# Conditioning and projection in one block, a third buffer of query weights, and another split of the 128 expert groups

## What is computed

```python
def reference(...):
    sh1, sc1, g1, sh2, sc2, g2 = split(c @ w_ada + b_ada, 6)
    h = rms(x, norm1_g) * (1 + sc1) + sh1
    q, k, v, logf, u = in_proj(h @ w_in)             # QK norm, log sigmoid, GLU
    a_out = forgetting_attention(q, k, v, cumsum(logf))
    c_out = silu(layernorm(causal_depthwise_conv(u, 31 taps)))
    x1 = x + g1 * (concat(a_out, c_out) @ w_o)
    h2 = rms(x1, norm2_g) * (1 + sc2) + sh2
    q = (h2 @ w_query).reshape(n, 8, 2, 128)          # 8 heads, two halves
    s = einsum(q, sub_keys)                           # 2 x 128 keys a head
    i1, i2 = top16(s[:, :, 0]), top16(s[:, :, 1])
    e = top16 of the 16 x 16 sums                     # 16 of 16384 experts, a head
    act = gelu(einsum(h2, expert_u[e]))
    y = x1 + g2 * einsum(softmax(top) * act, expert_v[e])
```

## Time and profile before

| what | value |
|---|---|
| runs | 3864.44, 3870.56, 3872.29 us (median 3870.56) |
| the profiled execution | 3873.22 us, its span 3871.5 us |
| busy: PE, DVE, ACT, POOL | 3115.4, 2471.7, 1550.2, 1283.3 us |
| mean granted clock of PE | 0.908 of full speed |
| DMA | 1291.75 MB in 299720 packets, mean 334 GB/s |
| gathers (q0) | 1124.27 MB, 72.3% of the 16 engines' span |
| SP's DMAs (q1) | 164.51 MB, 12.9% |
| first product of block 0's scores | 652 us |
| scores of blocks 4, 5, 6 begin at | 1920, 2293, 2660 us |

### The profile page before, as it was taken

How to read it: one execution, slowest core, us unless ns; L and a number is a source line. 1 busy time by engine, 2 the same in 40 slices (tenths; PEclk the granted TensorE clock), 3 DMA queues, 4 the chain that set the end, 5 groups by cost and what they waited for, 6 DMA issues and landing times.

```text
span 3871.5 us, 44083 instructions
## 1 busy us (share of the span) xinstructions
PE 3115.4 (80%) x11624; PEld 1421.8 (37%) x11624; DVE 2471.7 (64%) x6411; ACT 1550.2 (40%) x4275; POOL 1283.3 (33%) x1139
## 2 busy tenths in 40 slices
PE   8699976578887887788688868887887788757877
PEld 2466742333342243224332433343334333411341
DVE  0222323488588677767776777587668766856785
ACT  0234411246425533543355345534552555233423
POOL 0000030034334343444344334443343334344433
PEclk9699987699998998899899989998998899979989
DMA  8211152389999999999999999999999999989998
GB/s 317 86 47 41 41 200 96 132 320 399 367 376 366 414 404 375 371 413 407 371 401 409 408 355 404 408 401 378 400 398 403 341 407 405 380 338 418 417 377 355
DMA packets 299720, 1291.75 MB, mean 334 GB/s; under 512 B 39270, under 2 KB 135414, under 8 KB 163124
## 3 DMA queue, kind: packets, MB, share of 16 engines
q0 software_dynamic: 156672, 1124.27, 72.3%
q1 hardware_dynamic: 142780, 164.51, 12.9%
HBM read 1271.34 MB, written 17.79 MB: 333 GB/s over the span
## 4 chain that ended last, share of the span: by engine, by line
DMA 34%; PE 21%; DVE 14%; issue 7%; ACT 5%; SPq 1%; POOL 1%; DVEq 0%; POOLq 0%; ACTq 0%
DMA ring<-experts_dram,idxc 22%; DMA wq<-w_query_dram 12%; PE YY L1670 12%; DVE ring L1515 5%; PE M L1651 4%; PE TT L1657 3%; DVE yac L1262 2%; SPq L1021 1%; ACT gw L1229 1%; ACT dg L1237 1%; ACT L1227 1%; DVE yac L1436 1%; PE SS L1546 1%; ACT ga L1227 1%; POOL ring L1108 1%
## 5 line engine op out<-in xcount | busy, mean ns | idle before, releaser
L1670 PE MATMUL YY<-ring,dg 128*64 128x512 f32 (+1 forms) x4224 | 1804.1, 655 | 486.0 <-ACT dg L1237 463.3
L1108 POOL DMA_INDIRECT ring<-experts_dram,idxc x1056 | 1233.4, 1168 | 1810.3 <-PE YY L1670 1608.0
L1515 DVE CUSTOM_DVE_ANT_0 ring<-ring,h2c 128x1024 f32<-128x1024 f32 x1056 | 1273.3, 1226 | 551.6 <-DMA ring<-experts_dram,idxc 542.2
L1670 PEld LDWEIGHTS YY<-ring,dg 128*64 128x64 f32 (+1 forms) x4224 | 502.1, 145 | 1576.3 <-ACT dg L1237 831.2
L1227 ACT ACTIVATE ga<-act 128x1 f32<-128x1 f32 x1056 | 210.6, 199 | 911.5 <-DVE act L1515 909.1
L1651 PE MATMUL M<-fT,wq 128*128 128x128 f32 (+1 forms) x2304 | 310.2, 299 | 96.3 <-DMA wq<-w_query_dram 96.3
L1237 ACT ACTIVATE dg<-fold,gw 128x64 f32<-128x64 f32 x1024 | 356.0, 348 | 51.0 <-ACT gw L1229 2.6
L1651 PEld LDWEIGHTS M<-fT,wq 128*128 128x128 f32 x2304 | 297.4, 213 | 155.7 <-DMA wq<-w_query_dram 122.4
L1229 ACT ACTIVATE gw<-ga,gc 128x1 f32<-128x1 f32 x1056 | 311.0, 295 | 35.1 <-ACT ga L1227 1.0
L1262 DVE SCALAR_TENSOR_TENSOR yac<-win,cw,yac 128x128 f32<-128x128 f32 x960 | 262.9, 346 | 2.5 <-issue 2.5
L1188 ACT ACTIVATE qh<-M 128x256 f32<-128x256 f32 x64 | 24.5, 383 | 462.4 <-PE M L1651 462.4
(11 more groups left out here) (305 smaller groups left out, 2385.9 us busy)
## 6 DMA issues: line engine op xcount, KB each, us to landing
wq<-w_query_dram SPq DMA_DIRECT2D x72, 1024.0 KB, 27.0
wa<-w_ada_dram SPq DMA_DIRECT2D x12, 2048.0 KB, 7.9
ring<-experts_dram,idxc POOLq DMA_INDIRECT x1056, 13.7
w_in<-w_in_dram SPq DMA_DIRECT2D x1, 10272.0 KB, 34.1
kh<-kT_scratch SPq DMA_DIRECT2D x16, 264.0 KB
xb<-x_prompt_dram SPq DMA_DIRECT2D x8, 512.0 KB, 5.3
t_xb<-x_prompt_dram SPq DMA_DIRECT2D x8, 512.0 KB, 11.1
w_o<-w_o_dram SPq DMA_DIRECT2D x8, 512.0 KB, 5.5
```

What stands on the lines that cost most here:

```text
L1108: pool.indirect_dma_start(ring[:, k % RING, :], None, I["experts"], bass.IndirectOffsetOnAxis(idxc[:, k:k + 1], 0)).then_inc(g_in[k % RING ...
L1515: v.tensor_tensor_reduce(out=u, in0=u, in1=h2, scale=1.0, scalar=0.0, op0=ALU.mult, op1=ALU.add, accum_out=act8[:, k % RING:k % RING + 1]) ...
L1670: mm = pe.matmul(YY[o, half * 512:(half + 1) * 512], dg[:, k % DG, 0:w], ring[:, k % RING, D + half * 512:D + (half + 1) * 512], start=(k ...
```

## The change

There are three parts.

1. `condition` and `project` become one block, `front`. `condition` now returns pieces which `front` puts into each engine's stream. Its PSUM tiles are those of the projection (A[0] to A[4]), its row buffer is `sqq`, its gate buffers are `qTb` and `kTb`. The loads of `w_in` are cut: 8 parts for q, k, v and forget logits (0.79 MB each) stand between the last 8 chunks of `w_ada`, the part for GLU (4.2 MB) behind them. The norm of the sampled rows stands ahead of the conditioning. The gates are now transposed as 9 rows (16 transposes for the 32 products), the spreading into `gS` is gone, and a DMA repeats a gate's one row to 128 rows (from one SBUF partition) or a sample's row to 4. PE waits, ahead of the first q product, until DVE has copied the gates out of PSUM; ACT waits, ahead of its first write to `qTb`, until they are stored.
2. A third buffer for `wq`. It shares its memory (`shared`) with the two `kh` buffers. A load now waits for the product three heads before; that of head 2 waits for the block's last scores, and the next block's prefetch of keys for the product of head 5.
3. `PLAN`: 36 groups stand beside attention (were 50), 29 beside the middle (as before), 63 beside routing (were 49). Behind `write_indices` stand 4 + 3 + 2 = 9 groups (were 3 + 2 + 1 = 6).

```diff
-def condition(nc, I, S, K, w_in_load):
...
-            sp.dma_start(K["w_in"][:, :, :], I["w_in"].rearrange("(k p) n -> p k n", p=P)).then_inc(w_in_load, 16)
...
-            to_columns(NCH - 1)
-            pe.wait_ge(own_v, 1)
-            pe.wait_ge(id_step, 6)
-            for g, first in ((0, 16), (1, 40)):
-                for half in range(2):
-                    for c in range(4):
-                        mm = pe.matmul(gate_ps[2 * g + half][:, c * P:(c + 1) * P],
-                                       modT[:, first + 4 * half + c, 0:1].to_broadcast([P, P]),
-                                       ident[:, :], start=True, stop=True)
-            mm.then_inc(gates, 1)
-            pe.wait_ge(gates_out, 1)
-            for g, first in ((0, 16), (1, 40)):
-                for half in range(2):
-                    for c in range(4):
-                        mm = pe.matmul(gate_ps[2 * g + half][0:TS, c * P:(c + 1) * P],
-                                       gS[:, g, 4 * half + c, :],
-                                       ident[:, :], start=True, stop=True)
-            mm.then_inc(gates, 1)
...
-                for c in range(DC):
-                    fr = modT[:, (16, 40)[i] + c, 1:M].unsqueeze(2).to_broadcast([P, NS, QS])
-                    own.do(v.tensor_copy(gS[:, i, c, :].rearrange("p (n q) -> p n q", n=NS), fr))
...
+def condition(nc, ctx, I, S, K, R):
...
+    A, mod, gate = R["A"], R["mod"], R["gate"]
+    mod_ps = A[4][:, 0:48 * M].rearrange("p (n m) -> p n m", m=M)
+    row_ps, gate_ps = A[0:3], A[0:4]
...
+            if n >= NCH - DC:
+                k = n - NCH + DC
+                sp.dma_start(K["w_in"][:, k, 0:ZG], wi[:, k, 0:ZG]).then_inc(R["w_qkv"], 16)
+        sp.dma_start(K["w_in"][:, :, ZG:DIN], wi[:, :, ZG:DIN]).then_inc(R["w_glu"], 16)
+        sp.wait_ge(id_step, 7)
+        sp.dma_start(S["mask"], wide[:, :]).then_inc(gates_out, 16)
...
+            if n:
+                to_columns(n - 1)
+        rows_up(0)
+        to_columns(NCH - 1)
+        pe.wait_ge(own_v, 1)
+        for g, first in ((0, 16), (1, 40)):
+            for half in range(2):
+                for c in range(4):
+                    mm = pe.transpose(gate_ps[2 * g + half][0:M, c * P:(c + 1) * P], modT[:, first + 4 * half + c, :],
+                                      ident[:, :])
+        mm.then_inc(modT_done, 1)
+    def vector_rows(v):
+        for n in range(NCH):
+            v.wait_ge(w_used, n + 1)
+            if n >= 2:
+                v.wait_ge(modT_done, n - 1)
...
+    def vector_gates(v):
+        v.wait_ge(modT_done, NCH + 1)
+        for g in range(2):
+            for half in range(2):
+                v.tensor_copy(gate[g][0:M, half * 512:(half + 1) * 512], gate_ps[2 * g + half][0:M, :])\
+                    .then_inc(rows_copied, 1)
+    def store_gates(sp):
+        sp.wait_ge(rows_copied, NCH + 4)
+        for g in range(2):
+            sp.dma_start(S["gate"][g].unsqueeze(0), gate[g][0:1, :].unsqueeze(1).to_broadcast([1, P, D]))\
+                .then_inc(gates_out, 16)
+            sp.dma_start(S["gate_s"][g].rearrange("(n q) d -> n q d", q=QS),
+                         gate[g][1:M, :].unsqueeze(1).to_broadcast([NS, QS, D])).then_inc(gates_out, 16)
+    def gates_stored(eng):
+        eng.wait_ge(gates_out, 16 * 5)
+    def modulation_ready(eng):
+        eng.wait_ge(own_v, 5)
+    def gates_read(eng):
+        eng.wait_ge(rows_copied, NCH + 4)
+    return (sync, gpsimd, tensor, vector_rows, vector_gates, store_gates, gates_stored, modulation_ready, gates_read)
...
+def front(nc, I, O, S, K):
...
+        w_qkv, w_glu = sem("p_wqkv"), sem("p_wglu")
+        flat = lambda a: a[:, :, :].rearrange("p h t -> p (h t)")
+        c_sync, c_gpsimd, c_tensor, c_rows, c_gates, store_gates, gates_stored, modulation_ready, gates_read = condition(
+            nc, ctx, I, S, K, {"A": A, "mod": sqq[:, :].rearrange("p (g n) -> p g n", g=2),
+                               "gate": [flat(qTb), flat(kTb)], "w_qkv": w_qkv, "w_glu": w_glu})
             sp.dma_start(xb[0:TS, :], I["x_sample"]).then_inc(x_in, 16)
+            c_sync(sp)
...
             load_x(1, 0)
+            store_gates(sp)
             store(0, 1, None, None)
...
                 if not isinstance(t, int) or t > 0:
                     act.wait_ge(stored_qk, 32 * t)
+                else:
+                    gates_stored(act)
...
+            norm_x(0)
             act.wait_ge(own_p, 5)
-            norm_x(0)
             body(0, 0)
...
                 if r == TS:
+                    c_rows(v)
...
                     v.sem_inc(hT_ready, 1)
+                    c_gates(v)
                 if more:
                     norm_x(t + 1)
+                if not some(t):
+                    v.wait_ge(own_p, 5)
+                    v.wait_ge(small_in, 80)
...
-            v.wait_ge(own_p, 5)
-            v.wait_ge(small_in, 80)
+            norm_x(0)
+            body(0)
...
                 if some(t):
                     pe.wait_ge(qkT_ready, t)
+                else:
+                    gates_read(pe)
...
+                if not some(t):
+                    pe.wait_ge(w_glu, 16)
                 gated(1, r, h)
...
-            pe.wait_ge(w_in_load, 16)
-            rows_up(0)
+            c_tensor(pe, rows_up)
+            pe.wait_ge(w_qkv, 16 * DC)
             body(0, 0)
...
-PLAN = [3] * 14 + [4] * 2 + [2, 1, 1, 1, 2, 2, 1, 1, 2, 2, 2, 2] + [2, 1, 1, 1, 1, 2, 2] + [3, 3] + [2, 3] * 8 + [2, 1]
+PLAN = [2, 2, 2, 3] * 4 + [2, 1, 1, 1, 2, 2, 1, 1, 2, 2, 2, 2] + [2, 1, 1, 1, 1, 2, 2] + [4, 4] + [3, 3] * 7 + [4, 4] + [3, 2]
...
-        wq = [sb(f"wq{i}", [P, DC, 2 * NK]) for i in range(2)]
+        shared = sb("shared", [P, 2 * SEQ])
+        wq = [sb(f"wq{i}", [P, DC, 2 * NK]) for i in range(2)] + [shared[:, :].rearrange("p (k n) -> p k n", k=DC)]
         subk = sb("subk", [P, H, 2, NK])
         V = sb("V", [P, NB, DA])
-        kh = [sb(f"kh{i}", [AUG, SEQ]) for i in range(2)]
+        kh = [shared[0:AUG, i * SEQ:(i + 1) * SEQ] for i in range(2)]
...
             def load_wq(t, h):
-                n = H * t + h
-                if n >= 2:
-                    sp.wait_ge(qd_done, n - 1)
-                sp.dma_start(wq[n % 2][:, :, :], wqv[:, :, h * 2 * NK:(h + 1) * 2 * NK]).then_inc(wq_in[n % 2], 16)
+                b = h % 3
+                if h > 2:
+                    sp.wait_ge(qd_done, H * t + h - 2)
+                elif b == 2:
+                    sp.wait_ge(s_done, H * min(t + 1, NB))
+                elif t:
+                    sp.wait_ge(qd_done, H * t - 1 + b)
+                sp.dma_start(wq[b][:, :, :], wqv[:, :, h * 2 * NK:(h + 1) * 2 * NK]).then_inc(wq_in[b], 16)
...
                     sp.wait_ge(s_done, H * t)
                     sp.wait_ge(m_ready, H * t)
                     sp.wait_ge(conv_done, t)
+                    sp.wait_ge(qd_done, H * t - 2)
                 sp.dma_start(qTb[:, :, :], S["qT"][:, :, t * P:(t + 1) * P]).then_inc(q_in, 16)
...
-                    pe.wait_ge(wq_in[h % 2], 64 * t + 16 * (h // 2 + 1))
+                    b = h % 3
+                    pe.wait_ge(wq_in[b], 16 * ((2 if b == 2 else 3) * t + h // 3 + 1))
                     for g in range(2):
                         for k in range(DC):
-                            mm = pe.matmul(M0[:, g * P:g * P + r], wq[h % 2][:, k, g * NK:(g + 1) * NK], fT[:, k, 0:r],
+                            mm = pe.matmul(M0[:, g * P:g * P + r], wq[b][:, k, g * NK:(g + 1) * NK], fT[:, k, 0:r],
```

171 lines of the change are left out of this document (68 added, 103 removed).

## The result

| | before | changed |
|---|---|---|
| median of the runs | 3867.5 us (3860.8 to 3872.3, 4 runs) | 3813.7 us (3811.9 to 3815.6, 4 runs) |
| first product of block 0's scores | 652.0 us | 619.1 us |
| block 1 (first score to first score) | 301.8 us | 281.1 us |
| blocks 2 to 6 together | 1860.8 us | 1866.0 us |
| block 7's first score to the end | 831.1 us | 820.1 us |

The ratio is 0.9862, 95% interval 0.9845 to 0.988: 53 us faster (46 to 60), where I had said 64 against the median of the first runs. The rows of the table already say that the sum came out and its middle did not. The five steady blocks 2 to 6, for which I had booked most of the third buffer's gain, are no faster.

What follows compares the result with a forecast made beforehand. Transfers bound the kernel from the first full block on, not before (yardstick 410 GB/s). Front 34.2 + buffer 24 + turn 19 - attention 14 = 63.2 off 3873.2 gives 3810.0, or 3807 us for the median; range 3772 to 3843.

Steps and rivals of the forecast that it cites:

- Front, 34.2 us: Before the tail: first q product at 108.6 us instead of 141.3, plus 1.5 from PE's clock; bounds 29 to 36.
- The cover of the `w_in` parts: Loads between the last `w_ada` chunks: two buffers of slack hide them, costed at nothing; 1.6 us if the cover were gone.
- Third buffer, 24 us: Routing: `wq` loads arrive in time, saving 4.0 us in each of blocks 1 to 6; between nothing and 36.
- I take the whole of the mean dip, 4.0 us, for blocks 1 to 6: Routing: transfer time lost below 410 GB/s, 6.0 us in block 4 and 2.0 in block 5, all recovered: 24 us.
- the 30.85 us of the earlier trace: Routing: one `wq` load on the chain, read as PE waiting, its sums stopping and POOL issuing no gathers.
- Turn, 19 us: Between blocks: POOL's 4.41 us wait for indices goes, shortening the transfer gap over 8 turns; between nothing and 38.
- Half of the mean 4.7 over 8 turns: Between blocks: half of the mean transfer time lost per turn (8.0, 4.7 and 1.5 us) is recovered, 19 us.
- What is late next is the first sum of the next block: Between blocks: POOL's 14.40 us wait for that sum remains, untouched by the change, though the ring is fuller.
- Attention, 14 us lost: Attention with 14 fewer groups: PE needs slightly longer than transfers, 2 us a block over 7 blocks; nothing to 13.6 a block.
- My two terms for the split: Moving groups out of attention: 19 us gained at the turns between blocks, 14 us lost in attention.
- the blocks do not get faster: Blocks: transfers lost in one place are lost in another, so only the front counts; 3836 us, chance 17%.
- my signs of being wrong: Attention over 113 us, PE waiting more on diagonals or exponential, unchanged period, first `qTb` write after 165 us, or `wa` waits.

Runs made afterwards that it cites:

- part 1 alone: The kernel before with only conditioning and projection merged into one front block, without the rest of the change: 3833.3 us, ratio 0.9903.
- parts 1 and 3: The kernel before with the merged front and the new split of groups, but two `wq` buffers instead of three: 3818.2 us, ratio 0.9884.

## Why the prediction was right, and where it was not

- **Front, 34.2 us: right.** 32.9 us at the tail's first score, 34.7 with part 1 alone (single traces scatter by some us: that score stands at 615 to 622 us in the kernels with part 1 and at 649 to 652 in those without), and 37 (32 to 43) by the ratio of part 1 alone. That the start of the q product came within 0.3 us is partly luck: everything from the first chunk on was 1.6 us late, which no term of mine has, and the steps behind the last chunk took 1.3 us less than worked out. With part 1 alone these steps took 8.2 us again and the q product began at 107.65. The cover of the `w_in` parts, costed at nothing, held.
- **Third buffer, 24 us: wrong**, nothing within 3.5 us alone, and 5 to 8 us by the ratios beside the split, with 9 either way. The step that failed is "I take the whole of the mean dip, 4.0 us, for blocks 1 to 6": I read a rate under 410 GB/s as time lost to the wait ahead of it. In one of the two windows that made the mean (370 GB/s in block 5) the DMA share was 0.99: nothing was held back, the bytes were dearer. In the other 3.2 us were idle where I had 6.0. And the 30.85 us of the earlier trace rows are how long that load was under way; no wait of PE for `wq` was longer than 10.0 us in the whole kernel. Even the idle time that was there did not go: with parts 1 and 3, blocks 2 to 6 have 37 us of it without the buffer and 38 with it. In which places it came back isn't traced one by one. A wait for a load in a saturated queue is a wait for the queue.
- **Turn, 19 us: wrong.** POOL no longer waits for the indices (1.7 us in all for 41.0), as forecast, but the step "Half of the mean 4.7 over 8 turns" failed: at the turn behind block 4 the hole did not shrink, it grew from 4 to 10 us. "What is late next is the first sum of the next block", which I named, is still the larger part: where a loop goes back, DVE and ACT stand at the turn, and with part 1, for which I had no such term, a second stall of 5.2 us stands on DVE there.
- **Attention, 14 us lost: not seen.** 107.5 us in block 4 for my 104.0, within the bounds, but the whole split left blocks 2 to 6 where they were (1859.3 for 1860.8 alone). The shares over 1 in its rows say why: the transfers bound it, not PE.
- **Not in the sum: block 1.** 13 of the 19 us that the split gave. My two terms for the split were net 5; they should have been worked out per block, from the rows of the thin one.
- **The rival "the blocks do not get faster"** was the true mechanism of blocks 2 to 6: a period of 373.2 for 372.2, where I had 366 to 369. Two of my signs of being wrong came true, the period that has not changed and PE waiting more on ACT's diagonals (561 for 463 us). Its 3836 was missed only because block 1 and the last blocks are no steady blocks. The forecast's 3807 against 3813.7 is a right number partly by luck: of the 53 us some 34 rest on the reason given and about 20 on another.

## What to carry to other kernels

Price a wait by what the resource that sets the pace did during it: if the DMA share stayed at 1, removing the wait gives nothing, and if it fell, the idle time is the most it can give. Follow the freed work to the next pause before booking even that. Measure each part of a change alone before blaming one of them for a pause; a part can lengthen a pause that has nothing to do with its purpose. Where a list of shares is applied to blocks of different size, work out the odd block by itself; it may be the only one that is not at the limit. And read the stalls marked issue at loop turns: if an engine on the refill path stands there, writing the loop out can be worth more than any buffer.

## What the hardware showed unexpectedly

- At a branch back over a block's code, DVE and ACT each stood 4.8 to 5.7 us before their first instruction in the changed kernel (side by side, 14.5 and 15.8 us over three turns), and not where a block followed in line. The Trainium skill ("Runtime: NRT & Kernel Launch", Instruction fetch mechanics) says that a taken branch to code outside the fetched pages stalls the engine for a fetch; the runs agree in that without the branches both rows are gone, and with them 24 to 28 us of the kernel's time, part of which has no cause shown. That the stalls are fetches is the page's account; no row of a trace names a fetch.
- The gates' stores, each from one SBUF partition or eight, ran at 25 to 28 GB/s in all, for some 40 us; the issue of the second gate's store on SP took 15.17 us (0.59 for the first).
- 1 KB pieces on the hardware queue beside 8 KB gathers cost their bytes at 338 to 360 GB/s, not at 410. While keys came from scratch the gathers' own packets ran at 338 GB/s with the engines busy, and at 413 once that was over.
